# Reordering the end of the S5 stage: powers, kernel products, Z conversion and the token order

## What is computed

```python
h = rmsnorm(x, mix_norm[0])
# 64 groups of 16 inputs, each with a 64-dimensional complex diagonal state
bu = einsum("blgh,gph->blgp", h_grouped, bbar)
hs = associative_scan(state[t] = abar * state[t-1] + bu[t])
y  = real(einsum("blgp,ghp->blgh", hs, c)) + d * h
z  = gelu(y)
x  = x + (z @ w_ga) * sigmoid(z @ w_gb)
```

## Time and profile before

| what | value |
|---|---|
| median of 3 runs | 2537.57 us (2535.74 to 2539.46) |
| the profiled execution, its own time | 2535.47 us |
| its span, first to last instruction | 2533.5 us |
| mean granted TensorE clock | 0.984 of full |
| busy share of PE, DVE, ACT, POOL | 96%, 49%, 21%, 26% |
| DMA over the span | 69 GB/s mean |

### The profile page before, as it was taken

One profiled execution on the slowest core, in us unless ns is written; L12 is line 12 of the kernel. 1 busy time (PEld: TensorE's weight loads), 2 busy tenths in 40 slices (PEclk: granted clock), 3 DMA queues, 4 the chain that ended last, 5 costly groups with the idle time before them and its releaser, 6 DMA issues.

```text
span 2533.5 us, 41245 instructions
## 1 busy us (share of the span) xinstructions
PE 2426.7 (96%) x16662; PEld 2357.6 (93%) x16662; DVE 1246.8 (49%) x2172; ACT 544.0 (21%) x1109; POOL 658.4 (26%) x373
## 2 busy tenths in 40 slices
PE   6679999999999999999999899999999999999998
PEld 6669999999999999999999766689999999999998
DVE  8995234343333343456433677755344343333336
ACT  4434122000000000022100367743100000000003
POOL 0005323223333223322332100043223322333220
PEclk9889999999999999999999999999999999999999
DMA  3146111111111111112347355211111111111101
GB/s 116 31 98 210 39 45 51 36 49 50 50 51 42 42 50 50 50 34 76 101 145 213 120 146 152 68 34 42 42 51 50 42 42 50 50 50 50 38 30 68
DMA packets 87283, 174.79 MB, mean 69 GB/s; under 512 B 33994, under 2 KB 49866, under 8 KB 87122
## 3 DMA queue, kind: packets, MB, share of 16 engines
q1 hardware_dynamic: 78210, 156.60, 19.7%
q10 hardware_dynamic: 8912, 15.79, 2.0%
HBM read 148.54 MB, written 21.46 MB: 67 GB/s over the span
## 4 chain that ended last, share of the span: by engine, by line
PE 86%; DVE 4%; ACT 3%; DMA 2%; issue 2%; SPq 2%; ACTq 1%; POOL 0%; DVEq 0%; POOLq 0%
PE pair L1695 83%; PE pair L2110 1%; DMA kpg<-cache_k 1%; PE pair L1861 1%; DVE nmx L1543 1%; ACTq L398 1%; PE pair L1853 1%; DVE wmix L1573 1%; DMA X<-x_t 1%; DVE acc L1040 0%; SPq L391 0%; DVE kpg L1040 0%; DVE stok L1136 0%; ACT act_hi L663 0%; ACT prob L974 0%
## 5 line engine op out<-in xcount | busy, mean ns | idle before, releaser
L1695 PE MATMUL pair<-act_hi,w_hi 128*128 128x344 f32 x3264 | 1048.9, 321 | 7.6 <-DVE w_lo L1040 4.2
L1695 PE MATMUL pair<-act_hi,w_lo 128*128 128x344 f32 x3264 | 1043.7, 320 | 0.0
L1695 PE MATMUL pair<-act_lo,w_hi 128*128 128x344 f32 x3264 | 1043.3, 320 | 0.0
L1695 PEld LDWEIGHTS pair<-act_hi,w_hi 128*128 128x128 f32 x3264 | 616.1, 189 | 8.6 <-DVE w_lo L1040 4.4
L1695 PEld LDWEIGHTS pair<-act_hi,w_lo 128*128 128x128 f32 x3264 | 615.6, 189 | 0.0
L1695 PEld LDWEIGHTS pair<-act_lo,w_hi 128*128 128x128 f32 x3264 | 614.2, 188 | 0.0
L597 POOL CAST w_hi<-w_raw 128x1024 fp32r<-128x1024 f32 x178 | 205.5, 1154 | 1518.1 <-issue 689.1
L600 POOL TENSOR_TENSOR w_lo<-w_raw,w_hi 128x1024 fp32r<-128x1024 f32 x178 | 436.1, 2450 | 32.1 <-POOL w_hi L597 32.1
L1040 DVE TENSOR_TENSOR gate<-pair,R 128x344 f32<-128x344 f32 x132 | 68.2, 516 | 611.2 <-PE pair L1695 611.2
L1040 DVE TENSOR_TENSOR X<-X,pair 128x344 f32<-128x344 f32 x528 | 259.1, 509 | 189.4 <-PE pair L1695 189.2
L1695 PE MATMUL pair<-hid_lo,w_hi 128*128 128x344 f32 x1056 | 338.6, 321 | 0.0
(11 more groups left out here) (248 smaller groups left out, 1853.2 us busy)
## 6 DMA issues: line engine op xcount, KB each, us to landing
w_raw<-w SPq DMA_DIRECT2D x180, 512.0 KB, 3.3
kpg<-cache_k SPq DMA_DIRECT2D x16, 512.0 KB, 5.8
vpg<-cache_v SPq DMA_DIRECT2D x16, 512.0 KB, 7.5
qd<-qt SPq DMA_DIRECT2D x28, 256.0 KB, 5.3
ublk<-x_b SPq DMA_DIRECT2D x8, 576.0 KB, 8.1
X<-x_t SPq DMA_DIRECT2D x3, 1376.0 KB, 9.6
vt<-stage ACTq DMA_DIRECT2D x8, 516.0 KB, 6.8
z<-zblk SPq DMA_DIRECT2D x32, 128.0 KB, 3.2
```

The lines of the kernel that those rows point to most:

```text
L1695: return t_.matmul(out, lhsT, rhs, start=start, stop=stop)
```

## The change

What is computed does not change. The parts:

1. `powers(1)` moves ahead of `states(0)` on VectorE, and `powers(q + 2)` comes after `sines(q + 1)`. G is so ready a part earlier.
2. On TensorE `kernels(q)` is no longer run after `outputs_s5(q - 1)` but in the middle of `inputs(q)`, between its two halves; each half waits for its own `s5_ti`. `outputs_s5(q)` waits in addition for the next part's Kc copy.
3. On ScalarE `kernel_out` is cut in `kernel_copy` and `kernel_rows` (the DMAs into TM, now after the Gelu of the part before), and `tables(q + 1)` stands before the kernel's copy.
4. On SyncE the DMAs into TM go ahead of the stores of the part before. Weight units 0 and 1 and Z 0 and 1 are loaded in part 2 after `states(2)`; Z 2 to 5 in two pieces in part 3, units 2 and 3 between them; Z 6 and 7 and X as before. The final states are stored after the last outputs instead of ahead of them.
5. ScalarE converts units 0 and 1 and k 0 to 3 before the last part's Gelu, k 4 and 5 and the samples in the middle of it. VectorE converts right behind `states(3)`; the three small instructions for lambda come after that.
6. `first_glu` waits per k and unit, and for the Gelu only when it needs banks 4 and 5.
7. Tokens are kept in another order in every activation tile (`token_order`): within each 128 tokens by step within a block first. `z_high` and `z_low` write runs of 16 adjacent values in place of values 8 apart. The causal mask and the position table follow; the host reorders inputs and outputs. No instruction is added to the attention.
8. Tiles of the S5 stage are placed elsewhere in SBUF. GpSimd clears `bpad` only after `bbar` has been made (`s5_bb`), since `bpad` now lies on `b_in`; `padded(0)` on ScalarE waits for that.

The core of the diff:

```diff
+        BPAD_AT = rx[0]
+        b_in = place("b_in", [P, 2, PAIRS, 16], F32, rx)
+        bpad = nc.alloc_sbuf_tensor_at("bpad", [P, 2, 2, PP, 2, 16], F32, offset=BPAD_AT)
+
+        HI_AT, LO_AT = RAW_AT + 16384, RAW_AT + 2 * 16384
+        W_p = [nc.alloc_sbuf_tensor_at(f"W_{n}", [P, PP, L, 16], F32, offset=at)
+               for n, at in (("rr", HI_AT), ("ii", HI_AT + 4096), ("ri", LO_AT), ("ir", LO_AT + 4096))]
+        rh, rl = [HI_AT + 8192, HI_AT + 16384], [LO_AT + 8192, LO_AT + 16384]
...
+        def by_step(ap):
+            return ap.rearrange("p (i s b) -> p s i b", s=L, b=P // L)
+
+        def by_place(ap):
+            return ap.rearrange("p (s i b) -> p s i b", s=L, b=P // L)
...
                 for n in range(0, L, 2):
                     load_blocks(sp, n)
+                if q:
+                    sp.wait_ge(s5_gelu, 8 * q)
+                    for s in range(L):
+                        store_z(sp, q - 1, s)
+                    store_samples(sp, q - 1)
+                if q == PARTS - 2:
+                    sp.wait_ge(s5_h, 2 * (PARTS - 1))
+                    for r in range(2):
+                        sp.dma_start(w_raw[:, r, :], d["w"][r]).then_inc(w_in[r], 16)
+                    sp.wait_ge(s5_vs, PARTS)
+                    sp.wait_ge(z_out, 144)
+                    sp.dma_start(Z[:, 0:2], z_k[:, 0:2]).then_inc(z_in[0], 16)
                 if q == PARTS - 1:
-                    sp.wait_ge(z_out, 144 * (PARTS - 1))
-                    sp.wait_ge(s5_vs, PARTS)
-                    sp.dma_start(Z[:, 0:2], z_k[:, 0:2]).then_inc(z_in[0], 16)
+                    sp.wait_ge(z_out, 144 * (PARTS - 2))
+                    sp.wait_ge(s5_g, 2 * PARTS)
+                    sp.wait_ge(s5_k, 2 * PARTS)
+                    sp.dma_start(Z[:, 2:4], z_k[:, 2:4]).then_inc(z_in[1], 16)
                     sp.wait_ge(t_in, 256 * PARTS)
                     sp.wait_ge(s5_sb, PARTS)
-                    sp.wait_ge(s5_h, 2 * (PARTS - 1))
-                    for r in range(4):
+                    for r in range(2, 4):
                         sp.dma_start(w_raw[:, r, :], d["w"][r]).then_inc(w_in[r], 16)
-
-
-                    sp.wait_ge(s5_fin, 1)
-                    sp.dma_start(Z[:, 2:6], z_k[:, 2:6]).then_inc(z_in[1], 16)
-                    sp.dma_start(d["ssm_p"], fin[:]).then_inc(ssm_out, 16)
-                    sp.dma_start(d["ssm_s"], hs[:]).then_inc(ssm_out, 16)
-                if q < PARTS - 1:
-                    sp.wait_ge(s5_gelu, 8 * q + 8)
+                    sp.wait_ge(z_out, 144 * (PARTS - 1))
+                    sp.dma_start(Z[:, 4:6], z_k[:, 4:6]).then_inc(z_in[2], 16)
+                    sp.wait_ge(s5_gelu, 8 * PARTS)
                     for s in range(L):
                         store_z(sp, q, s)
                     store_samples(sp, q)
-                else:
-                    sp.wait_ge(s5_gelu, 8 * q + 8)
-                    for s in range(L):
-                        store_z(sp, q, s)
-                    store_samples(sp, q)
+                    sp.wait_ge(s5_fin, 1)
+                    sp.dma_start(d["ssm_p"], fin[:]).then_inc(ssm_out, 16)
+                    sp.dma_start(d["ssm_s"], hs[:]).then_inc(ssm_out, 16)
             sp.wait_ge(z_out, 144 * PARTS)
-            sp.dma_start(Z[:, 6:8], z_k[:, 6:8]).then_inc(z_in[2], 16)
-
-            sp.wait_ge(z_in[2], 16)
+            sp.dma_start(Z[:, 6:8], z_k[:, 6:8]).then_inc(z_in[3], 16)
+
+            sp.wait_ge(z_in[3], 16)
...
-            g.memset(bpad[:], 0.0).then_inc(s5_pad, 1)
             g.memset(dI[:], 0.0).then_inc(s5_pad, 1)
             for Hq in H:
                 g.memset(Hq[:, :, :, NS:NS + 1].rearrange("p x a o -> p (x a) o"), 0.0).then_inc(s5_nul, 1)
             g.memset(TM[:], 0.0).then_inc(s5_zero, 1)
+            pool.wait_ge(s5_bb, 2)
+            g.memset(bpad[:], 0.0).then_inc(s5_pad, 1)
...
+            def kernel_rows(q):
                 act.wait_ge(s5_kc, 2 * q + 2)
                 if q == 0:
                     act.wait_ge(s5_zero, 1)
+                else:
+                    act.wait_ge(s5_y, 8 * q)
...
             def z_high(k):
-                act.wait_ge(z_in[0 if k < 2 else 1 if k < 6 else 2], 16)
-                a.activation(act_hi[:, k, 0:SEQ].rearrange("p (b s) -> p s b", s=L),
-                             Z[:, k, 0:SEQ].rearrange("p (s b) -> p s b", s=L), ACT.Copy).then_inc(z_hi, 1)
+                act.wait_ge(z_in[k // 2], 16)
+                a.activation(by_step(act_hi[:, k, 0:SEQ]), by_place(Z[:, k, 0:SEQ]), ACT.Copy).then_inc(z_hi, 1)
...
             for q in range(PARTS):
                 if q + 1 < PARTS:
                     padded(q + 1)
                     turned(q + 1)
+                    initial(q + 1)
+                    tables(q + 1)
+                    kernel_copy(q + 1)
                     samples(q + 1)
+                if q == PARTS - 1:
+                    weight_high(0)
+                    weight_high(1)
+                    act.wait_ge(s5_g, 2 * PARTS)
+                    act.wait_ge(s5_sb, PARTS)
+                    act.wait_ge(s5_y, 8 * (PARTS - 1))
+                    for k in range(0, 4):
+                        z_high(k)
                 gelu(q, 0, 4)
                 if q == PARTS - 1:
-                    act.wait_ge(s5_fin, 1)
-                    z_high(0)
-                    z_high(1)
+                    for k in range(4, 6):
+                        z_high(k)
+                    z_samples(0, 6)
                 gelu(q, 4, 8)
                 if q + 1 < PARTS:
-                    kernel_out(q + 1)
-                if q + 2 < PARTS:
-                    tables(q + 2)
-            act.wait_ge(s5_y, 8 * PARTS)
-            act.wait_ge(s5_k, 2 * PARTS)
-            weight_high(0)
-            weight_high(1)
-            z_samples(0, 6)
-            for k in range(2, 6):
-                z_high(k)
+                    kernel_rows(q + 1)
             z_samples(6, KT)
...
             sines(0)
             weights(1)
             inputs(1)
+            powers(1)
             for q in range(PARTS):
                 states(q)
-                if q + 1 < PARTS:
-                    powers(q + 1)
                 if q + 2 < PARTS:
                     weights(q + 2)
                     angles(q + 2)
                     inputs(q + 2)
                 if q + 1 < PARTS:
                     sines(q + 1)
-
-            lv = lamv[:].rearrange("p (a b) n -> p a b n", a=2)
-            c.step(tt(lv[:, :, 0, :], lv[:, :, 0, :], lv[:, :, 1, :], ALU.mult))
-            c.add(v_.tensor_scalar(gsub[:], gsub[:], 1.0 - LAM_INIT, None, ALU.mult))
-            v_.reduce_sum(lamt[:, 0:2], lv[:, :, 0, :], axis=AXX).then_inc(lam_done, 1)
-
+                if q + 2 < PARTS:
+                    powers(q + 2)
...
-            z_low(0)
-            z_low(1)
+            dve.wait_ge(s5_y, 8 * (PARTS - 1))
             for u in range(2):
                 dve.wait_ge(w_hi_done, u + 1)
                 tt(w_lo[:, u, :], w_raw[:, u, :], w_hi[:, u, :].bitcast(F32), ALU.subtract).then_inc(w_split, 1)
+                z_low(u)
             z_samples(0, 6)
             for k in range(2, 6):
                 z_low(k)
+            lv = lamv[:].rearrange("p (a b) n -> p a b n", a=2)
+            c.step(tt(lv[:, :, 0, :], lv[:, :, 0, :], lv[:, :, 1, :], ALU.mult))
+            c.add(v_.tensor_scalar(gsub[:], gsub[:], 1.0 - LAM_INIT, None, ALU.mult))
+            v_.reduce_sum(lamt[:, 0:2], lv[:, :, 0, :], axis=AXX).then_inc(lam_done, 1)
...
                 pe.wait_ge(s5_rt, 4 * q + 4)
-                if q:
-                    pe.wait_ge(s5_ti, 2 * q)
                 for m in range(2):
+                    if m:
+                        kernels(q)
+                    if q:
+                        pe.wait_ge(s5_ti, 2 * q - 1 + m)
                     for pp in range(4):
                         for x in range(2):
                             for g2 in range(2):
                 if q == 0:
                     pe.wait_ge(s5_small, 4)
                 for r in range(2):
-                    if q:
-                        pe.wait_ge(s5_gelu, 8 * (q - 1) + r + 5)
                     for x in range(4):
                         pi = 4 * r + x
                         out = bank[4 + r][0:32, x * P:(x + 1) * P]
                 if q + 1 < PARTS:
                     pe.wait_ge(s5_vsc, q + 2)
                 pe.wait_ge(s5_nul, 2)
-                pe.wait_ge(s5_kc, 2 * q + 2)
+                pe.wait_ge(s5_kc, 2 * min(q + 1, PARTS - 1) + 2)
+                if q:
+                    pe.wait_ge(s5_gelu, 8 * q)
                 for it in range(4):
                     pe.wait_ge(s5_h, 2 * q + it // 2 + 1)
                     if it >= 2:
                         last.then_inc(s5_y, 1)
             inputs(0)
-            kernels(0)
             for q in range(PARTS):
                 if q + 1 < PARTS:
                     inputs(q + 1)
                 outputs_s5(q)
```

(13 more changed lines are left out.)

88 lines of the change are left out of this document (53 added, 35 removed).

## The result

| | before | after |
|---|---|---|
| median | 2535.12 us (8 runs, 2533.38 to 2539.46) | 2544.51 us (8 runs, 2539.79 to 2547.76) |
| ratio of comparable runs | 1 | 1.003, 95% interval 1.0021 to 1.0039 |
| profiled execution, own time | 2535.47 us | 2546.14 us |
| its span | 2533.5 us | 2544.1 us |
| mean granted clock | 0.984 | 0.980 |

What follows compares the result with a forecast made beforehand. VectorE bounds the S5 stage, TensorE the rest; the question is the second GLU tile's start and clock. Tile 1.7 us later (2.2 less 0.5) plus 2.35 restart gives 4.0 us: 2541.6 us, own range 2539 to 2544, stated range 2533 to 2547.

Steps and rivals of the forecast that it cites:

- the likeliest case: Whole kernel: a time within 0.2% (5.1 us) of the kernel before, chance 0.60; slower 0.30, faster 0.10.
- a VectorE wait of 3.6 us at `powers(3)`: Rival, middle of S5: slow output steps of part 1 make VectorE wait 3.6 us, giving 2545.2 us; chance 0.15.
- Z 2 and 3 hold ScalarE, that holds two output steps: Last part: Z lands at 185.9, Gelu starts at 187.9, TensorE starts steps 2 and 3 at 188.7 instead of 185.45.
- the last Gelu: End of S5 on ScalarE: ends at 196.3 against 194.1, 2.2 us later; bounds 193.6 to 197.6.
- nothing lost: VectorE in S5: work only reordered, same sum, so the last H stays at 185.45 if no new wait opens.
- in by about 190: SyncE's loads: Z 4 and 5 and units 2 and 3 landed by then, leaving a quiet stretch for the last stores.
- Stores, Z, X: From last Gelu to second GLU tile: stores gain 0 to 1 us, 0.5 taken; Z and X as before.
- The clock's restart: TensorE idles 6.6 us for X instead of 0.9, so the second GLU tile pays 2.35 us more at half clock.
- stays slow: Rival on ScalarE: new write pattern keeps two `z_high` at 1.97 us, adding 1.9 us, 2543.5 us; chance 0.12.
- VectorE without a gap: Expected sign in the trace: VectorE busy without a gap from 57 to 185.5 us, H complete at 185.5.
- The forecast's sum for part 1: Outputs of part 1 start at 120.7, take 9.1 us, end at 129.8, 4.2 us before `powers(3)` at 134.0.
- `bpad`'s clearing: Rival at the start: GpSimd's clearing waits for a VectorE gap and `states(0)` slips, 15.5 us, 2557; chance 0.03.

Runs made afterwards that it cites:

- the first repair: Changed kernel with Z 2 and 3 issued on SyncE right after the outputs of part 2, ahead of the TM DMAs; median 2542.17 us, ratio 1.002.
- the S5 matmuls: Changed kernel plus 12 extra identity matmuls in each part between kernel products and second half of input products; median 2544.13 us, ratio 1.0028.
- the experiment: Changed kernel plus 28 extra matmuls, result unused, between the first and second GLU tile; median 2543.47 us, ratio 1.0034.
- another version: Changed kernel with Z 2 and 3 early, later conversions, four stores from ScalarE's queue, and 12 extra matmuls before the second GLU tile; 2534.12 us, ratio 0.9993.

## Why the prediction was right or wrong

**The sign and the mechanism were right, the size was too small, and the likeliest case (no change that can be told) did not come.** Forecast 4.0 us; found 7.6 (ratio) to 9.4 (medians). The forecast's own range, 2539 to 2544, was missed. That 2544.51 lies within the stated 2533 to 2547 is partly luck: the range reached so far up for a VectorE wait of 3.6 us at `powers(3)`, which did not come in that form, and part of what filled the room has no step in the prediction. Between the two profiled executions the difference is 10.6 us: 5.1 up to the second tile, 2.9 at its restart, 2.6 in dips of the clock far behind. By its own steps:

- **Z 2 and 3 hold ScalarE, that holds two output steps: shown.** Moving the load alone, moving the conversions alone, and moving both each took the wait away, and with the last two the interval of the ratio lies below that of the changed kernel.
- **One step at 4.2 us, the other at 3.0: right.** The outputs ran from 191.11 to 198.42, 7.3 us for the forecast's 7.2.
- **The term that was mis-sized: the last Gelu.** Forecast 2.2 us later, measured 4.7 (194.11 to 198.85). The missing 2.5 us were there before the steps began: they were to start at 188.7 and started at 191.11. The step that failed is "nothing lost" on VectorE, with the outputs of part 2 ending at 168.4. VectorE waited 1.31 us at `powers(2)` and had started 0.8 us late, and those outputs ended at 170.7. SyncE's work followed them (TM at 170.75 and not at 168.4, Z 2 and 3 at 182.89 and not at 180.8, that is 12.1 us for the forecast's 12.4), and the landing took 5.47 us for 5.04.
- **Z 4 and 5 "in by about 190": wrong, and without a price here.** They were issued at 184.50 and landed at 194.1, 9.6 us later where the last piece of Z, of the same size, took 5.04, with Z 2 and 3 and two units under way at once. ScalarE waited 2.57 us for them in front of the last Gelus, but those had to wait for TensorE's last step all the same. It took away a good part of what the first repair gained: there this wait was 4.06 us and on the chain.
- **Stores, Z, X: -0.5 forecast.** From the last Gelu to the landing of the stores it took 8.4 us (198.85 to 207.2) after 8.9: as forecast. X took 13.93 us in place of 12.75, which adds 1.2. I had taken Z and X "as before". It was between 12.61 and 14.06 in the versions of the experiments, and 12.61 in the changed kernel with the S5 matmuls, so it is not shown that the 1.2 us are the change's.
- **The clock's restart: forecast 2.35, measured 2.9** in the trace (5.8 us at half clock); the experiment took it away, but its time does not give a price. The idle time is 7.05 us for 6.6. That the early conversions would be worth nothing because X is the cover held too: the first tile was done 7.05 us too early.
- **The price of the new layout: 1.0 us** per `z_high`, as taken; the rival "stays slow" (0.12) fell. VectorE's half fell from 2.02 to 1.22 us as well.
- **VectorE without a gap: wrong in part 0, right in part 1.** The rival had its wait at `powers(3)`, 3.6 us. In the profiled execution it was 1.31 us at `powers(2)`, one part earlier; in another version it was 1.69 at `powers(3)`. The forecast's sum for part 1, done for part 0, gives the same 4.2 us to spare, so it was not the missing sum but the clock in it: the outputs of part 0 began some 3.4 us later than that sum (86.43, against 78.2 + 4.0 and the 0.8 of the late start) and took 11.3 us instead of 9.1, with TensorE at half clock from the input products on. The outputs of part 1 ended 1.1 us ahead of `powers(3)`, not 4.2. So the rival's mechanism is real, of 1 to 2 us, comes and goes, and makes the larger part of the 2.1 us by which part 2 was late.
- **`bpad`'s clearing fell as a rival.** GpSimd's and VectorE's timelines after, to be set beside the earlier trace rows:

```profile
29.42 0.95 POOL L632 MEMSET bpad<- 128x1024 f32 x1 [26.32 <-DVE bbar L1069]
```

```profile
29.39 1.23 DVE L1069 TENSOR_TENSOR W_rr<-A_re,bbar 128x1024 f32<-128x1024 f32 x1
```

It takes 0.95 us beside a VectorE instruction with two inputs from SBUF. The Trainium skill, SBUF — State Buffer, section "Who interferes with whom", has only an instruction of GpSimd that reads SBUF blocked there; this row agrees.
- **The shift of 0.8 us at the start** (input loads) and the 2.6 us of late dips have no step in the prediction. Executions of the kernel before spread by 6 to 13 us in each set of runs, and a sum made against one of them carries that.

What stays open: how much of the difference of the medians is the restart. It could not be resolved by adding matmuls to the changed kernel (1.0 us, against 2.7 between two profiles). Nor is it shown that the late dips fall more often in the changed kernel: one profile of each says nothing on that.

## What to carry to other kernels

An engine's instruction that waits for a transfer holds everything behind it in program order: before work is moved forward into a gap, ask of every wait in it whether what stands behind it frees a buffer or starts a chain of transfers, and put such work (here Gelu, store) first. Where the next engine is held by the last transfer in a chain, speeding up other work only lengthens its pause, and pauses of 5.75 to 7.18 us on TensorE cost another 1.6 to 3.0 us at the restart here. If a moved group waits twice, do the sum of each wait: the second may be hidden until the first is repaired. And where an engine's spare time is a few microseconds, do its sum at both levels of the clock, for each pass of the loop.
